# Two feed-forward matrix products with 512-column matrix instructions, on one Trainium2 core

## The reference, cut to what matters

```python
x = x + mix @ w_out[l]
h = rms_norm(x, norm2_g[l])
x = x + jnp.square(jax.nn.relu(h @ w_ff1[l])) @ w_ff2[l]     # w_ff1 1024 x 4096, w_ff2 4096 x 1024
```

## Time and profile before

| | |
|---|---|
| Median of three runs | 1085.75 us (1085.55 to 1087.79) |
| Profiled execution, span | 1085.7 us |
| PE busy | 1042.7 us, 96%, 8145 products |
| DVE, ACT, POOL busy | 695.8, 610.4, 588.5 us |
| Chain that ended last | PE 73%, DVE 14%, ACT 6% |

### The profile page before, as it was taken

The page is one execution under the profiler, slowest core; times in us unless marked ns, Lnnn a source line. Parts: engine busy times, 40 slices in busy tenths (PEclk is TensorE's granted clock), DMA queues, the critical chain, the costliest instruction groups (busy, mean ns, idle before and its releaser), DMA issues.

```text
span 1085.7 us, 21365 instructions
## 1 busy us (share of the span) xinstructions
PE 1042.7 (96%) x8145; PEld 979.9 (90%) x8145; DVE 695.8 (64%) x1467; ACT 610.4 (56%) x1237; POOL 588.5 (54%) x448
## 2 busy tenths in 40 slices
PE   8999999999999999999999999999999998899896
PEld 8799988988889898989999999999899988889896
DVE  7869576666664425685485553332799976788864
ACT  5454557666665447764455655444434446568953
POOL 3656345454454459645534344346768875467652
PEclk9999899999999999999999999999999999999999
DMA  8234333333234442324555555555444543634442
GB/s 311 96 120 151 100 115 108 107 117 117 99 102 131 139 138 96 98 98 155 182 168 175 178 190 177 187 182 175 158 166 162 175 151 123 212 124 149 148 163 78
DMA packets 43157, 158.08 MB, mean 146 GB/s; under 512 B 4912, under 2 KB 4912, under 8 KB 42672
## 3 DMA queue, kind: packets, MB, share of 16 engines
q1 hardware_dynamic: 42912, 156.69, 43.5%
q10 hardware_dynamic: 144, 0.03, 0.0%
HBM read 155.65 MB, written 1.05 MB: 144 GB/s over the span
## 4 chain that ended last, share of the span: by engine, by line
PE 73%; DVE 14%; ACT 6%; issue 3%; POOL 2%; DMA 1%; DVEq 0%; ACTq 0%; SPq 0%; POOLq 0%
PE p_proj L1835 20%; PE p_proj L1836 19%; PE p_proj L1837 19%; PE p_score L1673 4%; PE p_proj L1820 3%; PE p_pv L1701 2%; DVE ring_lo L579 2%; ACT ring_hi L914 2%; DVE arena_r L1178 2%; PE p_turn L1683 1%; POOL ring_lo L579 1%; DVE arena L1399 1%; PE p_score L1593 1%; PE p_score L1741 1%; DVE arena_r L587 1%
## 5 line engine op out<-in xcount | busy, mean ns | idle before, releaser
L1835 PE MATMUL p_proj<-arena_r,ring_hi 128*128 128x256 f32 x2208 | 654.9, 297 | 18.8 <-POOL ring_lo L579 10.5
L1836 PE MATMUL p_proj<-arena_r,ring_hi 128*128 128x256 f32 x2208 | 626.7, 284 | 0.0
L1837 PE MATMUL p_proj<-arena_r,ring_lo 128*128 128x256 f32 x2208 | 626.3, 284 | 0.0
L579 POOL TENSOR_TENSOR ring_lo<-ring,ring_hi 128x1024 fp32r<-128x1024 f32 x178 | 427.9, 2407 | 291.7 <-ACT ring_hi L914 290.8
L1835 PEld LDWEIGHTS p_proj<-arena_r,ring_hi 128*128 128x128 f32 x2208 | 424.9, 192 | 38.1 <-issue 21.4
L1836 PEld LDWEIGHTS p_proj<-arena_r,ring_hi 128*128 128x128 f32 x2208 | 425.4, 193 | 7.4 <-issue 6.0
L1837 PEld LDWEIGHTS p_proj<-arena_r,ring_lo 128*128 128x128 f32 x2208 | 425.1, 193 | 0.0
L914 ACT ACTIVATE ring_hi<-ring 128x1024 fp32r<-128x1024 f32 x276 | 290.3, 1052 | 94.4 <-PE p_proj L1837 91.4
L579 DVE TENSOR_TENSOR ring_lo<-ring,ring_hi 128x1024 fp32r<-128x1024 f32 x98 | 125.1, 1276 | 71.9 <-ACT ring_hi L914 70.4
L688 POOL TENSOR_TENSOR sbuf_s<-sbuf_s,srow 128x256 f32<-128x256 f32 (+1 forms) x48 | 41.7, 870 | 83.1 <-DVE srow L1381 58.2
L937 ACT ACTIVATE arena_r<-arena 128x256 fp32r<-128x256 f32 x108 | 42.4, 409 | 39.8 <-DVE arena L1552 22.3
(11 more groups left out here) (287 smaller groups left out, 1163.9 us busy)
## 6 DMA issues: line engine op xcount, KB each, us to landing
ring<-w_stream SPq DMA_DIRECT2D x286, 512.0 KB, 3.3
arena<-w_tok SPq DMA_DIRECT2D x1, 1632.0 KB, 12.8
arena<-w_rgi SPq DMA_DIRECT2D x1, 1536.0 KB, 6.4
arena<-x_t SPq DMA_DIRECT2D x4, 256.0 KB, 6.5
arena<-w_cmp SPq DMA_DIRECT2D x1, 1024.0 KB, 15.7
out_t<-arena SPq DMA_DIRECT2D x4, 256.0 KB, 2.6
par<-cols SPq DMA_DIRECT2D x1, 323.0 KB, 3.3
row<-rows ACTq DMA_DIRECT2D x1, 32.0 KB, 3.5
```

The source lines that it names most:

```text
L579: return eng.tensor_tensor(ring_lo[:, u % RING, :, :].rearrange("p k n -> p (k n)"), ring[:, u % RING, :, :].rearrange("p k n -> p (k n)") ...
L1835: pe.matmul(slot(s)[:, 0:S], w_hi, hi, start=(c == 0), stop=False)
L1836: pe.matmul(slot(s)[:, 0:S], w_hi, lo, start=False, stop=False)
L1837: mm = pe.matmul(slot(s)[:, 0:S], w_lo, hi, start=False, stop=(c == n - 1))
```

## The change

In `ff1` and `ff2` the first two products of a block, which have the same weights, become one product with 512 columns: the chunk of rounded values and the chunk of remainders are its two halves, and the sums go to the two halves of the bank. A view `both` of the same memory gives the two chunks as one operand. The third product still adds into the first half.

Since the result is now the sum of the halves, DVE first adds them with a `tensor_reduce` that reads the bank as 256 pairs (`half_sums`). In `ff1` this writes FFR and frees the bank, and the positive part and the factor `rinv` follow in a second instruction, in place, which now announces `ffr_ready` to ACT. In `ff2` it writes a scratch tile `sqb`, and the add into XT reads that. The remainders of `ff` move from DVE to POOL. The other projections keep three products.

```diff
+HALVES = {"ff1": (XD, XD + 8), "ff2": (FFH, FFL)}
...
+        both = {name: under(f"both_{name}", [P, 2, lo - hi, S], (ARENA - hi) * S * 4)
+                for name, (hi, lo) in HALVES.items()}
...
-                 "h1": (lambda c: A(XT + c), lambda c: R(XD + c), lambda c: R(XD + 8 + c), None, "G"),
+                 "h1": (lambda c: A(XT + c), lambda c: both["ff1"][:, 0, c, :], lambda c: both["ff1"][:, 1, c, :], None, "G"),
...
-                 "ff": (lambda c: A(FFS + c % 4), lambda c: R(FFH + c), lambda c: R(FFL + c), "ffs_ready", "D"),
+                 "ff": (lambda c: A(FFS + c % 4), lambda c: both["ff2"][:, 0, c, :], lambda c: both["ff2"][:, 1, c, :], "ffs_ready", "P"),
...
+        def half_sums(key):
+
+            return slot(key).rearrange("p (a s) -> p s a", a=2)
...
                 elif k == "ffsq":
-                    was_read(act, ("job", "ff1", j), "D")
+                    act.wait_ge(sem("ffr_ready"), j + 1)
...
-                    dve.scalar_tensor_tensor(out=A(FFR + j % 4), in0=slot(job)[:, 0:S], scalar=0.0, in1=rinv[:, :],
+                    dve.tensor_reduce(A(FFR + j % 4), half_sums(job), AX.X, ALU.add)\
+                        .then_inc(read["proj", "D"], 1); note(read["proj", "D"])
+                    settle()
+                    dve.scalar_tensor_tensor(out=A(FFR + j % 4), in0=A(FFR + j % 4), scalar=0.0, in1=rinv[:, :],
                                              op0=ALU.max, op1=ALU.mult)\
-                        .then_inc(read["proj", "D"], 1); note(read["proj", "D"])
+                        .then_inc(sem("ffr_ready"), 1); note(sem("ffr_ready"))
...
+                    elif name in HALVES:
+                        link(dve.tensor_reduce(sqb[:, j % 2, :], half_sums(s), AX.X, ALU.add))
+                        dve.tensor_tensor(A(XT + j), A(XT + j), sqb[:, j % 2, :], ALU.add).then_inc(done, 1); note(done)
+                        dve.wait_ge(done, mine)
...
-                            pe.matmul(slot(s)[:, 0:S], w_hi, hi, start=(c == 0), stop=False)
-                            pe.matmul(slot(s)[:, 0:S], w_hi, lo, start=False, stop=False)
+                            if name in HALVES:
+                                pe.matmul(slot(s)[:, :], w_hi, both[name][:, :, c, :], start=(c == 0), stop=False)
+                            else:
+                                pe.matmul(slot(s)[:, 0:S], w_hi, hi, start=(c == 0), stop=False)
+                                pe.matmul(slot(s)[:, 0:S], w_hi, lo, start=False, stop=False)
                             mm = pe.matmul(slot(s)[:, 0:S], w_lo, hi, start=False, stop=(c == n - 1))
```

## The result

The kernel with the change takes **1091.86 us** (median of 5 runs, 1089.51 to 1094.04). The kernel before, run beside it, takes 1087.46 (5 runs). The ratio is 1.0053, with a 95% interval of 1.0040 to 1.0067. The change makes the kernel slower by about 5.8 us. The forecast was 1079.2, with a range of 1073.0 to 1086.5.

The account below looks back on a forecast made before the run. In `ff1` and `ff2` PE's pace was taken as the bound. PE's saving of -6.8 us, +0.1 at the start of `ff1` and +0.2 at the end of `ff2` gave -6.5: from 1085.7 to 1079.2 us, range 1073.0 to 1086.5.

Parts of the forecast that it names:

- The view of the bound: In `ff1` and `ff2` the time is PE's pace; DVE, ACT and POOL are busy only 30% to 58%.
- Term (1): PE in both stages: one product fewer in each of 512 blocks saves 13.3 ns a block, -6.8 us.
- The formula of the Trainium skill: PE, products back to back: N/2.4 + 2.5 ns each, so the merge saves only 1.3 us in all.
- term (5): End of `ff2`: the added reduction delays the last remainder, so PE waits about 0.1 to 0.2 us; +0.2 us.
- Term (3): DVE in `ff1`: reduction 0.69 us and second instruction 0.42 us a job, hidden behind PE; 0 us.
- a rival with 0.05: DVE in `ff1`: POOL holds instructions with two SBUF inputs by 1.85 us, 22 us slower there; 1104.6 us, chance 0.05.
- With PE leading, the phases are fixed: DVE and POOL in `ff1`: the second instruction ends at 600.99, POOL begins at 600.97, so only 0.8 us remainders can meet.
- (2): First job of `ff1`: its last block waits for a chunk's remainder, the faster blocks ahead wait longer; +0.1 us.
- (4): POOL in `ff1`: 32 value remainders of 0.80 us, 26 us on top of its 37.9, fit its idle time; 0 us.
- the 120 behind a 256-column product's start: Sign in PE's timeline in `ff1`: the start behind a 256-column product still comes at 120 ns.
- the 227 behind a 512-column one: Sign in PE's timeline in `ff1`: the start behind a 512-column product comes at 227 ns.
- The few holds and PE without gaps: Signs: DVE's second instruction at 0.42 to 0.5 us with few holds, and PE without gaps in both stages.

Follow-up runs that it names:

- experiment 4: The change plus five runs of 24 extra float32r products, 128 to 512 columns, into idle banks ahead of `val_glu`: 1112.66 us for one run.
- experiment 2: The change with the reduction's sum written to an idle PSUM bank, so the second instruction has one SBUF input: 1085.03 us, ratio 0.9971 to the kernel before.
- experiment 6: The change with ACT's square of `ff1` and that value's rounding one job later in the order: 1080.76 us, ratio 0.9950 to the kernel before.
- experiment 3: The change with 512-column products in `ff2` alone, `ff1` as before, value remainders still on POOL: 1086.31 us, ratio 0.9991 to the kernel before.

## Why the prediction was wrong

- **The view of the bound** was right: inside the stages the time was PE's pace, and DVE, ACT and POOL had room. With the change that ended in `ff1`.
- **Term (1), PE, -6.8 us.** The mechanism and price are right in a stream of equal products (experiment 4: 13.3 ns a product, 226.7 for the long one). In the stage the mix of long and short ran mostly at 353.3, so the term was worth -3.4 to -6.8: the stretch without any hold is 3.1 us shorter (experiment 2), 504 blocks of 6.7 ns less 0.2 for term (5). The formula of the Trainium skill (TensorE: Matmul & The Clock Gate, "Back-to-back issue gap"), by which it would have been -1.3, is not borne out: 226.7 ns for 512 columns is 13.3 over N/2.4, not 2.5. That section of the Trainium skill calls the formula the gap of an isolated product, a limit that the prediction left out, and has about 131 ns for N=512 in a stream of loads and products. The 226.7 ns measured here in such a stream, with float32r, do not agree with that figure either. One quotient of the working is off, without effect: (1.89 - 0.28) / 15 is 107 ns and not 108.
- **Term (3), DVE at nothing, is the step that failed.** The reduction came out at 0.69 as worked out. The second instruction was priced at 0.42, "held" only in a rival with 0.05. It was held in one job of two, by 2.05 us: just under the 2.1 us that the rival named as its threshold. That threshold counted only DVE's own work, 3.45 + 2.05 = 5.5 us, where PE takes 5.55 at 347 ns a block. So much does fit: in experiment 6 DVE has 2.0 us of holds in two jobs and PE isn't kept waiting. What it left out is who is queued behind the waiting work: the square waits for the second instruction, `ring_hi` stands behind the square, and the next `ring_lo` waits for `ring_hi`. The chain through two engines is 6.27 us long though neither engine is full. The rival saw the hold but gave it the wrong way to do harm, so its 22 us (both instructions held, DVE over PE's time) are not what came: the loop cost 9.5 us, of which PE's gain took back 3.1.
- **"With PE leading, the phases are fixed"** was the argument against it. The phase that it worked out does exist: in experiment 2, where the second instruction isn't held, it runs 600.68 to 601.10 and POOL begins at 601.09. But the stage doesn't begin in that phase: in the change, DVE finishes `rinv` only at 571.01, when PE is at the end of its second job, and POOL is at work from 570.18. The second instruction of the first job is held (1.10 us), and the loop is closed from the third on (576.36, 2.47 us). Whether the stage would stay free of holds if it began in the other phase was not tried.
- **Terms (2), (4), (5)** are right. The wait for the last remainder at the head of `ff1` went from 0.84 to 0.9 us; POOL's moved work costs nothing (experiment 3); at the end of `ff2` two starts of `val_glu` (758.43 and 758.68 in the change) have the next one 0.25 and 0.22 us behind them in place of 0.12, so 0.2 us as forecast. The wait of 1.80 us at the head of `ff2` belongs to the loop of (3) and was in no term.
- **The Trainium skill's rule on who interferes** (SBUF — State Buffer, "Who interferes with whom") was cited for the right rival. These runs agree with the first half: an instruction with two SBUF inputs that begins behind POOL's ends 0.28 us behind it. The earlier trace rows had shown the same (begun 0.35 behind, ended 0.28 behind). On the second half they show only a tensor_reduce that reads PSUM, never held in 32; one with its input in SBUF beside POOL was not run.
- Of the signs named, 7633 products, 0.69 us for the reduction and the 120 behind a 256-column product's start in a uniform stream came true; the 227 behind a 512-column one did too in a uniform stream, and was 230 to 241 in the mix. The few holds and PE without gaps did not. "I am wrong if PE's gaps in `ff1` name DVE or POOL" came true as well.

## What to carry to other kernels

When an instruction on VectorE changes from one SBUF input to two while GpSimd streams, give it the duration of GpSimd's instruction beside it, and then walk the whole chain behind it over the other engines' queues back to itself: the length of that loop, not each engine's busy time, is what must stay under TensorE's time. If it doesn't, put one operand in PSUM or move what is queued behind the held result one step later; either brought back some 9 us here. A phase in which two instructions miss each other is no cover unless the stage also starts in it.

## What the runs showed of the hardware that was not expected

- Alternating float32r products of 512 and 256 columns run at 346.7 or 353.3 ns a pair. The pace is taken up behind a start and kept until the next one, in experiment 2 over all of both stages; two products of each kind in turn run at 348.3 behind every start that was tried. What picks the pace is open.
- A float32r product with its weight load has 13.3 ns over its columns from 256 to 512 columns, and a floor of some 112 ns at 128. The columns in two pieces cost nothing.
- Being held is a matter of who comes first: 0.08 us ahead of GpSimd's instruction VectorE's keeps its 0.42 us, 0.21 behind it takes 2.47. In the first case GpSimd's takes 0.95 (experiment 6) in place of 0.73 to 0.76 (experiment 2).
